# High and low part as one operand of 512 columns in six output stages of a two-block transformer kernel

## The chip, the cores and the metric

The kernel runs on one core of a Trainium2 chip. The metric is the time of one execution in device microseconds. TensorE multiplies matrices, VectorE and ScalarE work elementwise, GpSimd and SyncE issue DMAs. TensorE's results land in PSUM, in banks of 512 numbers of 32 bits per partition.

## The reference

Two blocks of two layers each on 256 tokens of width 1024 (the first block's first layer also carries 256 context tokens). Layer by layer there are attention or a state-space mixer, an output projection, and an MLP; all in float32. What matters here are the products that are added to the residual h:

```python
h_lat = h_lat + ga1 * y_lat                     # y_lat = attention(...) @ swa_wo[j]
h_lat = h_lat + ga2 * squared_relu_mlp(modulate(rms_norm(h_lat, g_mlp[i]), sh2, sc2), mlp_w1[i], mlp_w2[i])
...
h = h + sb_mixer(rms_norm_2(h, b_norm[j]), b_w_q[j], b_q_norm[j], k, v, b_w_o[j])
h = h + conv_ffn(rms_norm_2(h, ffn_norm[layer]), ffn_w_up[layer], ffn_conv_w[layer], ffn_conv_b[layer], ffn_w_down[layer])
```

## The kernel before, in words

Channels lie on the 128 partitions, tokens along the columns. A weight matrix is cut into units of 1024 columns (512 KB): eight k-tiles of 128 x 128 for one output tile of 128 channels. All weights run in one order through a ring of four slots.

Precision comes from two parts: each float32 number x is split into a rounded part "hi" (type float32r) and the rest "lo". A product is hi*hi + w_hi*x_lo + w_lo*x_hi, three matmuls into the same columns of one bank (`products`, L724 to L732), each with a weight load of its own. With 256 tokens only half of the bank is used.

For each weight unit SyncE loads `raw` (`load_unit`), ScalarE rounds it to `w_hi` (`split_unit`, L1144; it waits until TensorE is done with the slot's last unit), VectorE subtracts to get `w_lo` (`lower`, L1576), TensorE waits for that (`lo`). ScalarE and VectorE run their queues strictly in order, so this work stands in one line with the work on the output tiles.

Stages are of kinds. "RES" stages are output projections whose result is added to h. Those on 256 tokens are wo1, wo2 (8 tiles of one unit, 8 k-tiles each), down1a, down1b (8 tiles of two units, 16 k-tiles) and fdown0, fdown1 (8 tiles of three units, 22 k-tiles). The order of the stages from wo1 on: wo1, norm, up1a, down1a, up1b, down1b, win, state-space mixer, glu, fup0, fdown0, k2, q2, v2, attention, wo2, fup1, fdown1, output. Tiles use banks 0 to 3 in turn; TensorE may start tile j when h of tile j - 4 has been updated.

In a RES stage VectorE does, per tile: the `lower` of the units that come three later (the one of every fourth tile's last unit after the tile, in stages with row sums), then the update of h (L1621 to L1635). wo1, down1a and down1b have a gate: one scalar_tensor_tensor, h = bank * gate + h (L1633). wo2 has none (L1629), and fdown0 and fdown1 first multiply the bank by `rsn` (L1628), then add. Stages with row sums (wo1, down1b, fdown0, wo2) go on per tile: ScalarE waits for h, makes the next stage's high operand (`next_hi`, L1243, not in wo1) and the square of h (L1187), and after these the next `split_unit`; VectorE makes the low operand (`next_lo`, L1672) and adds the square to `ssum` (L1717). At the end TensorE sums `ssum` and the last square over the channels (`row_total`, L828): for wo1 before the norm, for the others after the sixth k-tile of the next stage.

In down1a, up1b and down1b VectorE also makes tables for the state-space mixer (`tables`, L2096 to L2105), in parts at fixed units; TensorE multiplies them at fixed units too (`table_mid`, L638 and L651), two units after the part in these stages. A `link` is a semaphore increment by an instruction and a wait for it by the next one on the same engine.

fup1 (kind "UP") may start its first tile when the second last update of h in wo2 is done (`bank_free`).

## Time and profile before

| | |
|---|---|
| median of 3 runs (1707.87 to 1715.15) | 1713.21 us |
| span of the profiled execution | 1706.6 us |
| TensorE matmul busy | 1606.4 us, 94%, 11872 instructions |
| TensorE weight load busy | 1421.1 us, 83% |
| VectorE busy | 1308.7 us, 77%, 2229 instructions |
| ScalarE busy | 869.5 us, 51% |
| mean granted clock of TensorE | 0.982 |
| chain that ended last | PE 73%; DVE 18%; issue 4%; ACT 3%; DMA 2% |

PE is TensorE, DVE VectorE, ACT ScalarE. The span runs from the first to the last instruction of one execution that the profiler took; the runs' times are of other executions and hold what lies around the span too. Matmuls are pipelined: their durations overlap, so what one costs is read from the distance between two starts. The granted clock is the share of full speed (2.4 GHz) that TensorE was given; half of it is 1.2 GHz. "Idle before" is the idle time of the engine just before an instruction, with who ended it.

### The profile page before, as it was taken

How to read it: one execution, taken by the hardware profiler on the slowest of the kernel's cores; microseconds unless marked ns; L12 is line 12 of the kernel's file. 1: busy time of each engine (PE TensorE's matmuls, PEld its weight loads, DVE VectorE, ACT ScalarE, POOL GpSimd, SP SyncE). 2: the span in 40 equal slices, each digit the busy share in tenths (PEclk: the TensorE clock that was granted, in tenths of full speed). 3: DMA queues.
4: the chain of work that ended last, by engine and by line, in shares of the span. 5: the costliest groups of instructions: out<-in, count | busy, mean ns of one | idle time of the engine just before them, and what ended most of it. 6: DMA issues, size and time to landing. Idle time of an engine off the chain costs nothing.

```text
span 1706.6 us, 32698 instructions
## 1 busy us (share of the span) xinstructions
PE 1606.4 (94%) x11872; PEld 1421.1 (83%) x11872; DVE 1308.7 (77%) x2229; ACT 869.5 (51%) x1505; POOL 104.3 (6%) x174
## 2 busy tenths in 40 slices
PE   6999899899999999788989999889999999899999
PEld 3778666688888888674789999789999998699999
DVE  5899897788767867678677787777887686578874
ACT  4664386343213433566555555355555586555542
POOL 0001030000000023120000212000000000000000
PEclk9999999999999999998999999999999999999999
DMA  9246651345667855340156667735555644055554
GB/s 368 89 137 224 218 149 51 123 144 184 202 193 238 263 173 169 112 140 12 53 186 202 217 208 263 316 102 176 179 183 177 205 153 158 13 164 183 182 196 137
DMA packets 80828, 292.02 MB, mean 171 GB/s; under 512 B 10432, under 2 KB 12224, under 8 KB 78928
## 3 DMA queue, kind: packets, MB, share of 16 engines
q1 hardware_dynamic: 69552, 249.03, 44.4%
q0 software_dynamic: 11168, 41.54, 7.6%
q8 instruction: 69, 1.13, 0.3%
q14 instruction: 39, 0.32, 0.1%
HBM read 270.54 MB, written 18.68 MB: 169 GB/s over the span
## 4 chain that ended last, share of the span: by engine, by line
PE 73%; DVE 18%; issue 4%; ACT 3%; DMA 2%; ACTq 0%; DVEq 0%; SPq 0%; POOLq 0%
PE bank L730 22%; PE bank L732 21%; PE bank L731 21%; DVE stat L2121 2%; DVE w_lo L1576 2%; DVE prob L2140 1%; PE bank L914 1%; DVE bank L1588 1%; DVE ada_raw L1589 1%; PE bank L925 1%; DMA raw<-weights 1%; PE bank L940 1%; DVE qk L1771 1%; DMA ada_raw<-ada_w 1%; PE bank L818 1%
## 5 line engine op out<-in xcount | busy, mean ns | idle before, releaser
L730 PE MATMUL bank<-u_hi,w_hi 128*128 128x256 f32 (+1 forms) x1936 | 615.9, 318 | 31.2 <-DVE u_lo L1951 19.2
L731 PE MATMUL bank<-u_lo,w_hi 128*128 128x256 f32 (+1 forms) x1936 | 600.8, 310 | 0.0
L732 PE MATMUL bank<-u_hi,w_lo 128*128 128x256 f32 (+1 forms) x1936 | 600.8, 310 | 0.0
L1576 DVE TENSOR_TENSOR w_lo<-raw,w_hi 128x1024 fp32r<-128x1024 f32 x372 | 452.2, 1222 | 143.9 <-ACT w_hi L1144 131.4
L1144 ACT ACTIVATE w_hi<-raw 128x1024 fp32r<-128x1024 f32 x360 | 375.4, 1049 | 172.8 <-PE bank L732 142.7
L730 PEld LDWEIGHTS bank<-u_hi,w_hi 128*128 128x128 f32 x1936 | 372.5, 192 | 59.6 <-issue 35.7
L731 PEld LDWEIGHTS bank<-u_lo,w_hi 128*128 128x128 f32 x1936 | 372.8, 193 | 22.3 <-issue 3.8
L732 PEld LDWEIGHTS bank<-u_hi,w_lo 128*128 128x128 f32 x1936 | 372.6, 192 | 18.4
L730 PE MATMUL bank<-hid_hi,w_hi 128*128 128x512 f32 (+1 forms) x512 | 174.0, 340 | 0.0
L732 PE MATMUL bank<-hid_hi,w_lo 128*128 128x512 f32 (+1 forms) x512 | 172.1, 336 | 0.0
L731 PE MATMUL bank<-hid_lo,w_hi 128*128 128x512 f32 (+1 forms) x512 | 172.0, 336 | 0.0
L730 PEld LDWEIGHTS bank<-hid_hi,w_hi 128*128 128x128 f32 x512 | 97.1, 190 | 11.0 <-issue 1.5
L732 PEld LDWEIGHTS bank<-hid_hi,w_lo 128*128 128x128 f32 x512 | 97.1, 190 | 10.2
L731 PEld LDWEIGHTS bank<-hid_lo,w_hi 128*128 128x128 f32 x512 | 97.1, 190 | 9.7
L1589 DVE SCALAR_TENSOR_TENSOR ada_raw<-ada_raw,silu_row 128x1024 f32<-128x1024 f32 x80 | 97.7, 1222 | 9.3 <-DMA ada_raw<-ada_w 9.0
L730 PE MATMUL bank<-f_hi,w_hi 128*128 128x256 f32 x352 | 99.8, 283 | 0.0
L731 PE MATMUL bank<-f_lo,w_hi 128*128 128x256 f32 x352 | 99.6, 283 | 0.0
L732 PE MATMUL bank<-f_hi,w_lo 128*128 128x256 f32 x352 | 99.6, 283 | 0.0
L1195 ACT ACTIVATE rs<-bank 128x512 f32<-128x512 f32 (+1 forms) x64 | 31.3, 489 | 125.2 <-PE bank L732 118.7
L730 PEld LDWEIGHTS bank<-f_hi,w_hi 128*128 128x128 f32 x352 | 67.6, 192 | 0.2
L732 PEld LDWEIGHTS bank<-f_hi,w_lo 128*128 128x128 f32 x352 | 67.6, 192 | 0.0
L731 PEld LDWEIGHTS bank<-f_lo,w_hi 128*128 128x128 f32 x352 | 67.6, 192 | 0.0
(317 smaller groups left out, 2260.3 us busy)
## 6 DMA issues: line engine op xcount, KB each, us to landing
raw<-weights SPq DMA_DIRECT2D x372, 512.0 KB, 3.4
ada_raw<-ada_w SPq DMA_DIRECT2D x80, 512.0 KB, 4.1
ada_first<-ada_w SPq DMA_DIRECT2D x16, 512.0 KB, 14.4
bias_sb<-bias_na POOLq DMA_DIRECT2D x16, 256.0 KB, 3.4
toep_dram<-zeros POOLq DMA_DIRECT2D x8, 512.0 KB, 9.1
bat_dram<-bat POOLq DMA_DIRECT2D x16, 256.0 KB, 4.2
ca_dram<-ca POOLq DMA_DIRECT2D x16, 256.0 KB, 3.8
s_bat<-bat_dram POOLq DMA_DIRECT2D x4, 1024.0 KB, 8.2
```

What stands on the lines that cost most here:

```text
L730: pe.matmul(dst, wh, hi[:, kt, xs], start=first, stop=False)
L731: pe.matmul(dst, wh, lo[:, kt, xs], start=False, stop=False)
L732: return pe.matmul(dst, wl, hi[:, kt, xs], start=False, stop=final)
L818: pe.matmul(SUM_BANKS[b2][:, 0:s.tok], C("block"), sq[:, b2, 0:s.tok], start=True, stop=True).then_inc(S["p2"], 1)
L914: pe.matmul(psum[2 * (g % 2) + a][:, 0:keys], q_ap, k_ap, start=True, stop=True).then_inc(att_s, 1)
L925: mm = pe.transpose(psum[4 + a][:, t * P:(t + 1) * P], prob[:, 2 * (g % 2) + a, t * P:(t + 1) * P], C("ident"))
L940: mm = pe.matmul(psum[6 + pr % 2][a * HD:(a + 1) * HD, qt * P:(qt + 1) * P], heads[a][2][t], prob_t[:, 2 * (g % 2) + a, t * P:(t + 1) * P] ...
L1144: A(w_hi[:, slot, :], raw[:, slot, :], ACT.Copy).then_inc(S["hi"], 1)
L1195: chain.link(A(rs[:, b2, 0:s.tok], bank[:, 0:s.tok], ACT.Relu))
L1576: TT(w_lo[:, slot, :], raw[:, slot, :], w_hi[:, slot, :].bitcast(F32), ALU.subtract).then_inc(S["lo"], 1)
L1589: STT(raw_, raw_, 1.0, silu_row[:, 0, :], ALU.mult, ALU.mult, accum_out=ada_acc[:, b, a % 4, 0:1]).then_inc(S["ada_read"], 1)
L2121: red = dve.tensor_reduce(stat[:, 0, b, :], both[:, :, 0:keys], AX.X, ALU.max, negate=True)
```

## The change

In the six RES stages of 256 tokens the high and the low operand are addressed as one tensor with a leading dimension of two (`u_both`, `hid1_both`, `f_both`; the addresses stay the same). Under the high weight one matmul takes both, 2 x 256 columns, into the whole bank; the low weight's matmul adds hi's product to the upper half. So a k-tile has two matmuls and two weight loads in place of three and three. The two halves of the bank are added when h is updated: VectorE adds the upper half's product to h and then the lower half's, in two instructions with a link between them. In fdown0 and fdown1 the multiplication by `rsn` takes the whole bank of 512 columns, and two additions follow, both linked to what is before them.

```diff
--- before.py
+++ after.py
@@ -181,8 +181,8 @@
         big = cursor[0]
         cursor[0] += 64 * 1024
         u_at = cursor[0]
-        u_hi = place("u_hi", [P, KT, TOK], F32R)
-        u_lo = place("u_lo", [P, KT, TOK], F32R)
+        u_both = place("u_both", [P, 2, KT, TOK], F32R)
+        u_hi, u_lo = u_both[:, 0], u_both[:, 1]
         con = place("con", [P, N_CON])
         vec = place("vec", [P, N_VEC])
         adab = place("adab", [P, 2, N_ADA, 2])
@@ -234,8 +234,8 @@
         sb_w = place("sb_w", [P, 2, 2, 384], at=at_ + 6144)
         mask_r = place("mask_r", [P, 384], F32R, at=big + 40960)
         ident_r = place("ident_r", [P, P], F32R, at=big + 42496)
-        f_hi = place("f_hi", [P, FT, SEQ], F32R, at=big)
-        f_lo = place("f_lo", [P, FT, SEQ], F32R, at=big + FT * 1024)
+        f_both = place("f_both", [P, 2, FT, SEQ], F32R, at=big)
+        f_hi, f_lo = f_both[:, 0], f_both[:, 1]
         fx = big + 2 * FT * 1024
         f_c = place("f_c", [P, 2, SEQ], at=fx)
         f_sig = place("f_sig", [P, 2, SEQ], at=fx + 2048)
@@ -265,8 +265,8 @@
 
         HOME0 = table_home("0", u_at, (sq_at + 4096, sq_at + 12288), PAIRS // 2)
         HOME1 = table_home("1", big + 32768, (big + 32768 + 25600, big + 32768 + 30208), PAIRS // 2)
-        hid1_hi = place("hid1_hi", [P, HALF, SEQ], F32R, at=big)
-        hid1_lo = place("hid1_lo", [P, HALF, SEQ], F32R, at=big + 16384)
+        hid1_both = place("hid1_both", [P, 2, HALF, SEQ], F32R, at=big)
+        hid1_hi, hid1_lo = hid1_both[:, 0], hid1_both[:, 1]
         HID = {n: (hid_hi, hid_lo) for n in ("up0a", "up0b")}
         HID.update({n: (hid1_hi, hid1_lo) for n in ("up1a", "up1b")})
         assert cursor[0] <= nc.sbuf_usable_end, cursor[0] - nc.sbuf_usable_end
@@ -482,6 +482,7 @@
                     "v2": (("q2", ("a1", "a3")),)}
 
         MODS_NEEDED = {"mix0": 4, "mlp0": 10, "mix1": 16, "mlp1": 22}
+        BOTH = {"wo1": u_both, "wo2": u_both, "down1a": hid1_both, "down1b": hid1_both, "fdown0": f_both, "fdown1": f_both}
         VAL = {"v0": val0, "v1": val1, "v2": val2}
         QK_DST = {"qk0": qk0, "q1": q1, "k1": k1, "k2": k2, "q2": q2}
         QK_GAIN = {"qk0": ("gqk0", 0), "q1": ("gqk1", 0), "k1": ("gqk1", 8), "k2": ("gqk2", 0), "q2": ("gqk2", 8)}
@@ -727,6 +728,11 @@
                 wh, wl = w_hi[:, slot, t * P:(t + 1) * P], w_lo[:, slot, t * P:(t + 1) * P]
                 dst = TILE[(s.tile0 + jj) % RING][:, 0:s.tok]
                 xs = NORM_COLS.get(s.name, slice(0, s.tok))
+                if s.name in BOTH:
+                    bank = TILE[(s.tile0 + jj) % RING]
+                    pe.matmul(bank[:, :].rearrange("p (a t) -> p a t", a=2), wh, BOTH[s.name][:, :, kt, xs], start=first, stop=False,
+                              skip_group_check=True)
+                    return pe.matmul(bank[:, SEQ:2 * SEQ], wl, hi[:, kt, xs], start=False, stop=final, skip_group_check=True)
                 pe.matmul(dst, wh, hi[:, kt, xs], start=first, stop=False)
                 pe.matmul(dst, wh, lo[:, kt, xs], start=False, stop=False)
                 return pe.matmul(dst, wl, hi[:, kt, xs], start=False, stop=final)
@@ -1621,12 +1627,19 @@
                 elif s.kind == "RES":
                     dve.wait_ge(S["unit"], n_done)
                     gate = s.more.get("gate")
+                    lower_half = slice(SEQ, 2 * SEQ)
                     if gate is None:
                         part = bank
                         if s.name in HIDDEN:
                             part = tmp[:, b2, :]
-                            link(TT(part[:, all_], bank[:, all_], rsn[:, all_], ALU.mult))
+                            link(TT(part.rearrange("p (a t) -> p a t", a=2), bank[:, :].rearrange("p (a t) -> p a t", a=2),
+                                    rsn[:, all_].unsqueeze(1).to_broadcast([P, 2, SEQ]), ALU.mult))
+                        link(TT(dcol(h, j, all_), part[:, lower_half], dcol(h, j, all_), ALU.add))
                         TT(dcol(h, j, all_), part[:, all_], dcol(h, j, all_), ALU.add).then_inc(S["d1"], 1)
+                    elif s.name in BOTH:
+                        g = mod[:, gate[0], bass.ds(j + gate[1] * 8, 1), 0]
+                        link(STT(dcol(h, j, all_), bank[:, lower_half], g, dcol(h, j, all_), ALU.mult, ALU.add))
+                        STT(dcol(h, j, all_), bank[:, all_], g, dcol(h, j, all_), ALU.mult, ALU.add).then_inc(S["d1"], 1)
                     else:
                         for hf in range(s.tok // SEQ):
                             cs = slice(hf * SEQ, (hf + 1) * SEQ)
```

## Rows read from the trace of the kernel before

**Rows 1.** Busy time by stretch: wo1, down1a, down1b, wo2, fdown1. PE, PEld, DVE, ACT, POOL, clock, DMA.

```profile
834.90:858.30 23.40, 23.29 (x192) 23.09 (x192) 13.73 (x21) 9.15 (x15) 0.00 (x0) 1.00 0.44 137
...
912.80:962.30 49.50, 49.50 (x468) 48.81 (x467) 39.40 (x50) 23.47 (x38) 10.38 (x17) 1.00 0.71 224
...
1009.80:1057.70 47.90, 47.90 (x428) 47.52 (x427) 34.85 (x50) 24.59 (x42) 8.88 (x15) 1.00 0.66 213
...
1486.80:1510.20 23.40, 23.29 (x192) 23.09 (x192) 14.01 (x24) 10.71 (x19) 0.00 (x0) 1.00 0.41 135
...
1639.80:1703.40 63.60, 63.57 (x529) 63.36 (x528) 34.91 (x44) 23.66 (x25) 0.00 (x0) 1.00 0.53 170
```

**Rows 2.** TensorE in order of time, down1a. Start, duration, line, operands, idle before.

```profile
949.74 0.28 PE L732 MATMUL bank<-hid_hi,w_lo 128*128 128x256 f32 x1
...
959.10 0.28 PE L732 MATMUL bank<-hid_hi,w_lo 128*128 128x256 f32 x1
```

**Rows 3.** TensorE in order of time, down0a, 512 columns.

```profile
439.69 0.39 PE L732 MATMUL bank<-hid_hi,w_lo 128*128 128x512 f32 x1
...
445.81 0.39 PE L732 MATMUL bank<-hid_hi,w_lo 128*128 128x512 f32 x1
```

**Rows 4.** VectorE in order of time, wo2.

```profile
1507.03 0.42 DVE L1629 TENSOR_TENSOR h<-bank,h 128x256 f32<-128x256 f32 x1
...
1509.57 1.23 DVE L1576 TENSOR_TENSOR w_lo<-raw,w_hi 128x1024 fp32r<-128x1024 f32 x1 [1.39 <-ACT w_hi L1144]
...
1510.71 0.42 DVE L1629 TENSOR_TENSOR h<-bank,h 128x256 f32<-128x256 f32 x1
```

**Rows 5.** TensorE in order of time, first and fifth tile of fup1.

```profile
1511.18 0.39 PE L730 MATMUL bank<-u_hi,w_hi 128*128 128x256 f32 x1 [1.03 <-DVE h L1629]
...
1524.42 0.36 PE L730 MATMUL bank<-u_hi,w_hi 128*128 128x256 f32 x1 [0.40 <-DVE f_h L1737]
```

**Rows 6.** VectorE in order of time, wo1.

```profile
853.78 0.48 DVE L1633 SCALAR_TENSOR_TENSOR h<-bank,mod,h 128x256 f32<-128x256 f32 x1
...
857.00 0.48 DVE L1633 SCALAR_TENSOR_TENSOR h<-bank,mod,h 128x256 f32<-128x256 f32 x1
...
858.31 0.48 DVE L1633 SCALAR_TENSOR_TENSOR h<-bank,mod,h 128x256 f32<-128x256 f32 x1 [0.50 <-PE bank L732]
```

**Rows 7.** VectorE in order of time, two linked instructions on 255 and 254 columns.

```profile
1522.72 0.48 DVE L1732 SCALAR_TENSOR_TENSOR f_c<-f_g,vec,f_c 128x255 f32<-128x255 f32 x1
...
1523.24 0.48 DVE L1734 SCALAR_TENSOR_TENSOR f_c<-f_g,vec,f_c 128x254 f32<-128x254 f32 x1
```

**Rows 8.** VectorE in order of time, two linked tensor_tensor, fdown0.

```profile
1339.94 0.42 DVE L1628 TENSOR_TENSOR tmp<-bank,rsn 128x256 f32<-128x256 f32 x1
...
1340.39 0.43 DVE L1629 TENSOR_TENSOR h<-tmp,h 128x256 f32<-128x256 f32 x1
```

**Rows 9.** VectorE by line and form: name, count, busy, mean ns, idle.

```profile
L2205 DVE TENSOR_TENSOR x_mod<-bank,rot 128x512 f32<-128x512 f32 x4 | 2.7, 677 | 1.4 <-PE bank L1012 1.4
```

**Rows 10.** VectorE in order of time, down1b.

```profile
1033.92 0.48 DVE L1633 SCALAR_TENSOR_TENSOR h<-bank,mod,h 128x256 f32<-128x256 f32 x1 [0.29 <-PE bank L732]
...
1039.51 0.76 DVE L2103 SCALAR_TENSOR_TENSOR ca<-ca,tab_tmp 128x576 f32<-128x576 f32 x1
```

**Rows 11.** TensorE in order of time, down1b, unit 10.

```profile
1040.33 0.54 PE L651 MATMUL bank<-ca,tab_bbar 64*16 64x128 f32 x23
```

**Rows 12.** Busy time by stretch: around the start of up1a, and an idle stretch.

```profile
860.40:864.60 4.20, 0.00 (x0) 0.00 (x0) 3.17 (x8) 1.75 (x4) 0.20 (x1) 0.72 0.95 316
...
864.60:871.60 7.00, 6.96 (x42) 6.99 (x43) 5.83 (x14) 4.01 (x7) 0.00 (x0) 0.68 0.21 81
...
1082.50:1084.80 2.30, 0.01 (x2) 0.01 (x1) 1.81 (x3) 2.07 (x3) 0.47 (x1) 1.00 0.93 360
```

**Rows 13.** VectorE in order of time, start of k2.

```profile
1364.82 0.42 DVE L1717 TENSOR_TENSOR ssum<-ssum,sq 128x256 f32<-128x256 f32 x1
```

**Rows 14.** TensorE in order of time, row totals in k2.

```profile
1365.58 0.60 PE L828 MATMUL bank<-ssum,con 128*128 128x256 f32 x2
```

## Prediction

> **What bounds the kernel now.** I read three views. First the busy time of each engine, stage by stage [rows 1]: in five of the six stages that change (fdown0 is built like fdown1) TensorE is busy for the whole stretch, VectorE for 55 to 80% of it, the DMA engines for 41 to 71%. Second the order of time on TensorE [rows 2, 3]. What counts there is the distance between starts, since the durations overlap. With 256 columns, 949.74 to 959.10 us is 78 distances, 120.0 ns each. With 512 columns, 439.69 to 445.81 us is 27 distances, 226.7 ns each. The difference is 106.7 ns for 256 columns, which is 2.4 GHz. So every matmul with its weight load costs its columns and 13.3 ns besides. Third, the joints between stages, in order of time on VectorE and TensorE [rows 4 to 6, 10, 11]. They show what the share of busy time hides: in wo1 and wo2 a chain of VectorE and ScalarE is longer than TensorE's tile. The result update of a tile (h) lets ScalarE square h; only then, in its queue, does it split the next weight unit; VectorE subtracts the low part (1.23 us) and only then reaches the next tile's h. Updates of h stand 3.68 us apart in wo2 (1507.03 to 1510.71) and 3.22 us apart in wo1 (853.78 to 857.00), where TensorE needs 24 matmuls of 120 ns, 2.88 us. At the end of wo2 TensorE has run out of lead and waits 1.03 us for the second last h [rows 5].
>
> **What is removed on TensorE.** Per k-tile three pairs of load and matmul (360.0 ns) become one of 512 and one of 256 columns (226.7 + 120.0 = 346.7 ns). The columns stay, one fixed cost of 13.3 ns goes. K-tiles: wo1 and wo2 64 each, down1a and down1b 128 each, fdown0 and fdown1 176 each, 736 in all, 9.8 us if all of it arrived.
> No row shows a moving operand in two pieces (high and low lie apart). Bounds: nothing, as the 512 columns in one piece show [rows 3], or one more fixed cost of 13.3 ns, as if it were two matmuls. A gain has no reason, since each column must stream. I take nothing, the nearest row being the one of the same count of columns.
> The Trainium skill (TensorE: Matmul & The Clock Gate, "Back-to-back issue gap") gives an isolated gap of N/2.4 + 2.5 ns; by that the change would save 736 x 2.5 ns, an estimate of 1.8 us, not 9.8. The rows here show 13.3 ns at both widths, so the rule does not hold for these loads and matmuls; the forecast doesn't use it.
>
> **What is added on VectorE.** A gated update (wo1, down1a, down1b) gets a second scalar_tensor_tensor, linked to the first by a semaphore. Two such linked instructions start 0.52 us apart [rows 7]. In wo2 it is a second linked tensor_tensor; linked ones start 0.45 us apart [rows 8]. In fdown0 and fdown1 the scaling takes 512 columns in place of 256 (677 ns from PSUM, where 256 took 0.42 us [rows 8, 9], so +0.26 us) and a linked add, 0.45 us: +0.7 us a tile. The read of rsn twice over is taken at no cost, as the table operations that repeat an operand show nothing else at 512 columns; its upper bound would be another 0.3 us at two joints.
>
> **Stage by stage**, against the profiled execution.
> down1a: TensorE-bound [rows 1], VectorE 39.4 of 49.5 us busy; 8 x 0.52 = 4.2 us more leave it under 44 of 47.8 us. This stage takes no row sums, so ScalarE doesn't wait for h. All of the gain arrives: 128 x 13.3 ns = -1.7 us.
> down1b: here ScalarE does wait for h, and VectorE also makes the last state-space table, which TensorE needs in its unit 10. The table's last part ends at 1039.51 + 0.76 = 1040.27 us, TensorE takes it at 1040.33 us: no slack [rows 10, 11]. Three updates of h lie ahead of the fourth in that chain, 3 x 0.52 = 1.56 us, less 0.29 us that VectorE waited for TensorE there; with the fourth's own 0.52 us the table comes 1.8 us later. TensorE comes 82 k-tiles x 13.3 ns = 1.1 us earlier and stalls some 2.9 us. The stage gives +1.8 us up to there and -0.6 us on its last 46 k-tiles: +1.2 us. Bounds: -1.7 us, if the chain has slack between its tiles that I didn't see, and +1.8 us.
> wo1: the first update starts 0.1 us earlier (8 k-tiles). Up to the eighth update the chain has seven links of 0.52 us, 3.6 us; but the fourth tile's update waited for TensorE and its row sum for a square, and the eighth's waited 0.50 us for TensorE again, some 1.4 us of slack in all. 3.6 - 0.1 - 1.4: the last row sum comes 2.1 us later, and the norm and up1a wait for it. TensorE's 0.85 us are lost in this. +2.1 us; bounds +1.0 (half of the links hidden) and +3.1 (all eight links, 4.2 us, less 1.1 us).
> wo2: the same chain with 0.45 us a step. Seven links up to the end of the second last h are 3.2 us, less 0.1 us at the first tile and 0.5 us at the fourth, whose square is next on ScalarE only after a weight split and so hides one link: that h ends 2.6 us later, so fup1 starts 2.6 us later. The chain stays the last to end up to the fifth tile of fup1, where TensorE waits 0.40 us for VectorE [rows 5], so nothing is caught up. +2.6 us; bounds +1.3 and +3.4.
> The clock at that joint: wo2's last matmul would end 0.85 us earlier and fup1 start 2.6 us later, so TensorE's idle 1.03 us becomes some 4.5 us. In this trace, TensorE's idle stretch before up1a (4.3 us) came with the granted clock down to half, and in the 7 us after it the mean grant was 0.68; a stretch of 2.3 us left it at 1.00 [rows 12]. 0.68 means 4.5 us of the 7 at 1.2 GHz, where 256 columns take 213 ns (256 / 1.2 GHz) in place of 120: 44% of 4.5 us, 2.0 us, less the 0.40 us that TensorE waited there anyway: +1.6 us. I take it, as 4.5 us is nearer to 4.3 than to 2.3.
> fdown0: TensorE-bound, VectorE has room: 176 x 13.3 ns = -2.35 us. At its end the row totals need the last-but-one row sum, which ended at 1365.24 us, 0.34 us before TensorE took it [rows 13, 14]; 0.7 us more makes a stall of 0.4 us. -1.95 us.
> fdown1: -2.35 us, and the last tile's chain to the output +0.7 us in the open: -1.65 us.
> What moves otherwise: nothing; the operands keep their addresses, and no DMA or queue is passed. Each bank is freed 0.5 us later, with three further banks before TensorE wants it again.
>
> **Sum**: -1.7 + 1.2 + 2.1 + 2.6 + 1.6 - 1.95 - 1.65 = +2.2 us. The profiled span of 1706.6 us becomes 1708.8 us. The median of the runs, 1713.2 us, lies 6.6 us above the span; the same difference gives 1715.4 us. (A measurement of this kernel can tell about 0.5%, 8.6 us, from no change.)
>
> **Rivals.**
> The gain arrives whole: VectorE's additions are hidden, as its 77% of busy time suggests, except the last tile's 0.7 us: -9.8 + 0.7 gives 1704.1 us, just faster. Against it stand the steps of 3.68 and 3.22 us [rows 4, 6].
> The clock stays up at fup1: 1713.8 us. For it: the grant depends on more than the length of the gap.
> The clock falls also at the 2.9 us stall in down1b: 2.0 us more, 1717.4 us. Against it: the gap lies between a stretch of 2.3 us that was harmless and 4.3 us.
> Slower: the split operand. If each read in two pieces costs x more, TensorE pays 526 x, over the k-tiles where it is on the path (128 in down1a, 46 in down1b, 352 in fdown). At x = 13.3 ns that is 7.0 us, 1722.4 us, slower by 0.5%; it decides from x = 12 ns. For it: no row has such an operand. Against it: the cost of a matmul in this trace is columns and a fixed part.
> The two-figure rule of the page named above (2.5 ns) would be a rival of the same kind, with 19% of the gain on the path: 5.7 us of the 7.0 lost, 1721.1 us. I give it 0.03, since 120.0 and 226.7 ns speak against it.
>
> **How the numbers follow.** Forecast as summed 0.60; clock stays up 0.14; gain arrives whole 0.06; clock falls in down1b too 0.08; split operand 0.09; small fixed cost 0.03. Predicted: 1715.4 us. The forecast's own bounds: low with wo1 and wo2 at their lower ends and no stall in down1b, 1715.4 - 1.1 - 1.3 - 2.9 = 1710.1; high with the upper ends, 1715.4 + 0.9 + 0.8 + 0.6 = 1717.7. The runs of before spread by 5.3 us below and 1.9 us above their median, so I widen to 1707 below; above, I reach to the split operand, 1722.5. Faster 0.06, slower 0.10, within 0.5% 0.84.
>
> **What would show each step.** On TensorE: starts in the pattern 227 and 120 ns in fdown1, 61.2 us in place of 63.6 for the stage; 240 and 120 would be the split operand. On VectorE: updates of h 4.1 us apart in wo2 and 3.7 us in wo1; an idle stretch of TensorE of some 4.5 us ahead of fup1 with the granted clock at half behind it; a wait of TensorE for ca in down1b of about 2.9 us; the row total of wo1 2.1 us later relative to the stage's start. The forecast is wrong if wo1 and wo2 end when TensorE does, or if down1b runs through.

## The result and the profile after

| | median | runs | ratio to before |
|---|---|---|---|
| before | 1712.32 us | 16 | |
| after | 1719.25 us | 16 | 1.0041, interval 1.0031 to 1.0052 |

The change costs 7.0 us (interval 5.3 to 8.9 us). The forecast was 1715.4 us. The profiled execution of after spans 1716.8 us, in a run of 1718.94 us. So 2.1 us lie around a span, not the 6.6 us that the forecast carried along.

The table gives, from the order of time on TensorE, what each stage costs from its first start to the next stage's first start (in the last row, up to the end of the span), as the difference after minus before in microseconds. The first pair is the two traces that the case began with; the second pair is a further execution of each kernel (e9 and e11 below).

| stage | forecast | first pair | second pair |
|---|---|---|---|
| wo1 to the start of up1a | +2.1 | +2.11 | +2.03 |
| up1a (clock) | 0 | +0.57 | +0.56 |
| down1a | -1.7 | -1.03 | -1.06 |
| down1b | +1.2 | +1.39 | +1.38 |
| end of win to the start of glu | 0 | +3.61 | +2.77 |
| glu | 0 | +1.38 | +1.58 |
| fdown0 | -2.35 | -2.33 | -2.33 |
| k2 (wait for the row sum) | +0.4 | +0.72 | +0.73 |
| wo2 to the start of fup1 | +2.6 | +2.71 | +2.65 |
| fup1 (clock) | +1.6 | +0.58 | +0.63 |
| fdown1, and the chain to the output | -1.65 | -1.24 + 0.70 | -1.23 + 0.73 |

Without the two lines from win to glu these add up to +4.2 us (first pair) where +2.2 was forecast. The remaining 2.8 of the 7.0 us must lie where nothing was changed. Between the end of win and the end of glu both pairs show more than that, 5.0 and 4.4 us, but a third kernel with the whole change (e3) shows 1.2 us there, and much of it varies between executions, as told below. Other unchanged stages differ either way (the spans of the pairs differ by 10.2 and 6.0 us).

Busy time by stretch, kernel after, for wo1, down1a, down1b, wo2 (both up to the next stage's start) and fdown1; columns as in [rows 1]:

```profile
835.12:867.70 32.58, 23.73 (x133) 20.33 (x133) 23.42 (x42) 12.57 (x20) 2.03 (x3) 0.93 0.50 172
916.40:964.70 48.30, 48.30 (x339) 41.61 (x338) 42.59 (x57) 23.50 (x38) 10.25 (x16) 1.00 0.68 226
1012.30:1061.40 49.10, 46.94 (x298) 40.48 (x298) 38.10 (x57) 24.39 (x42) 8.88 (x15) 1.00 0.59 192
1493.60:1522.20 28.60, 23.75 (x134) 20.49 (x135) 19.31 (x36) 11.93 (x21) 0.00 (x0) 0.99 0.36 116
1650.60:1712.70 62.10, 62.10 (x353) 53.74 (x351) 38.53 (x51) 23.79 (x25) 0.00 (x0) 1.00 0.49 168
```

down1a and fdown1 are shorter than in [rows 1] and TensorE is still busy throughout: there the saved time arrives. down1b was run through before; now TensorE is idle for 2.16 of its 49.1 us and the stage is longer.

TensorE in order of time, after, in fdown0 and in fdown1:

```profile
1321.79 0.39 PE L733 MATMUL bank<-f_both,w_hi 128*128 128x512 f32 x1
1322.02 0.28 PE L735 MATMUL bank<-f_both,w_lo 128*128 128x256 f32 x1
1322.13 0.39 PE L733 MATMUL bank<-f_both,w_hi 128*128 128x512 f32 x1
...
1689.72 0.40 PE L733 MATMUL bank<-f_both,w_hi 128*128 128x512 f32 x1
1689.95 0.28 PE L735 MATMUL bank<-f_both,w_lo 128*128 128x256 f32 x1
1690.07 0.40 PE L733 MATMUL bank<-f_both,w_hi 128*128 128x512 f32 x1
1690.31 0.28 PE L735 MATMUL bank<-f_both,w_lo 128*128 128x256 f32 x1
1690.43 0.40 PE L733 MATMUL bank<-f_both,w_hi 128*128 128x512 f32 x1
```

In fdown0 the starts of one k-tile are 0.34 us apart, again and again: 230 + 117 = 347 ns, the forecast's sum. In fdown1 they are 0.35 and 0.36 us apart, by turns 241 + 120, 236 + 113 and 233 + 117 ns, 353 ns on average. So only half of the saving arrives there, and in down1a too.

VectorE in order of time, after: two updates of h in wo1, two in wo2 (each update is two instructions now, the rows are of the second), and the state-space table in down1b:

```profile
852.49 0.48 DVE L1642 SCALAR_TENSOR_TENSOR h<-bank,mod,h 128x256 f32<-128x256 f32 x1
...
856.24 0.48 DVE L1642 SCALAR_TENSOR_TENSOR h<-bank,mod,h 128x256 f32<-128x256 f32 x1
...
1043.73 0.76 DVE L2116 SCALAR_TENSOR_TENSOR ca<-ca,tab_tmp 128x576 f32<-128x576 f32 x1
...
1512.57 0.42 DVE L1638 TENSOR_TENSOR h<-bank,h 128x256 f32<-128x256 f32 x1
1515.11 1.22 DVE L1582 TENSOR_TENSOR w_lo<-raw,w_hi 128x1024 fp32r<-128x1024 f32 x1 [2.11 <-ACT w_hi L1150]
...
1516.70 0.42 DVE L1638 TENSOR_TENSOR h<-bank,h 128x256 f32<-128x256 f32 x1
```

Updates stand 4.13 us apart in wo2 and 3.75 us in wo1; 3.68 and 3.22 us were read before [rows 4, 6]. So the link's 0.45 to 0.53 us is paid in full at each of these steps, because VectorE waits for ScalarE's next weight split and that waits for h.

TensorE in order of time, after: at that table, at the first row total in k2, and at the joint from wo2 to fup1; then the busy time of three stretches, the end of the idle stretch and the start of up1a, the idle stretch ahead of fup1 and what follows that (the clock is the third figure from the end):

```profile
1044.54 0.33 PE L652 MATMUL bank<-ca,tab_bbar 64*16 64x128 f32 x8 [2.16 <-DVE ca L2116]
...
1372.57 0.48 PE L834 MATMUL bank<-ssum,con 128*128 128x256 f32 x1 [0.29 <-DVE ssum L1730]
...
1516.88 0.28 PE L735 MATMUL bank<-u_both,w_lo 128*128 128x256 f32 x1
1521.32 0.39 PE L736 MATMUL bank<-u_both,w_hi 128*128 128x256 f32 x1 [4.16 <-DVE h L1638]
```

```profile
862.00:872.50 10.50, 6.08 (x27) 5.58 (x28) 8.91 (x21) 4.70 (x11) 0.00 (x0) 0.55 0.49 176
...
1517.20:1521.40 4.20, 0.08 (x1) 0.08 (x1) 2.77 (x6) 1.76 (x3) 0.00 (x0) 1.00 0.37 125
1521.40:1526.00 4.60, 4.60 (x23) 4.50 (x24) 4.30 (x9) 3.41 (x6) 0.00 (x0) 0.63 0.34 114
```

The idle 1.03 us [rows 5] have become 4.16 us, and the granted clock behind them is 0.63 on average over 4.6 us, partly at 1.2 GHz. Ahead of up1a it is the same: 0.55 over the 10.5 us that hold the idle stretch's end and the stage's start, where 0.68 and 0.72 stood before [rows 12].

The table that came just in time [rows 10, 11] now keeps TensorE idle for 2.16 us, and in k2 TensorE waits for a row sum that was there before [rows 13, 14].

### The profile page after: what moved, and what is told of

Its sections match the earlier page's. It is cut to its first block, busy times and chain, and to the rows that moved or that the text cites. A ratio compares the mean times of both kernels' runs of the same rounds, so it can differ in the third digit from the quotient of the medians.

```text
span 1716.8 us, 31306 instructions
## 1 busy us (share of the span) xinstructions
PE 1604.1 (93%) x11136; PEld 1386.8 (81%) x11136; DVE 1332.5 (78%) x2277; ACT 870.5 (51%) x1505; POOL 104.3 (6%) x174
## 3 DMA queue, kind: packets, MB, share of 16 engines
q8 instruction: 65, 1.06, 0.3%
## 4 chain that ended last, share of the span: by engine, by line
PE 69%; DVE 20%; ACT 4%; issue 4%; DMA 2%; ACTq 0%; DVEq 0%; SPq 0%; POOLq 0%
PE bank L736 17%; PE bank L737 16%; PE bank L738 16%; PE bank L733 7%; PE bank L735 4%; DVE w_lo L1582 3%; DVE stat L2134 2%; DMA raw<-weights 1%; DVE prob L2153 1%; DVE bank L1594 1%; DVE ada_raw L1595 1%; ACT w_hi L1150 1%; PE bank L920 1%; PE bank L931 1%; PE bank L946 1%
## 5 line engine op out<-in xcount | busy, mean ns | idle before, releaser
L736 PE MATMUL bank<-u_both,w_hi 128*128 128x256 f32 (+1 forms) x1808 | 581.8, 322 | 32.9 <-DVE u_both L1964 18.8
L737 PE MATMUL bank<-u_both,w_hi 128*128 128x256 f32 (+1 forms) x1808 | 566.7, 313 | 0.0
L738 PE MATMUL bank<-u_both,w_lo 128*128 128x256 f32 (+1 forms) x1808 | 566.6, 313 | 0.0
L736 PEld LDWEIGHTS bank<-u_both,w_hi 128*128 128x128 f32 x1808 | 350.1, 194 | 61.0 <-issue 33.1
L737 PEld LDWEIGHTS bank<-u_both,w_hi 128*128 128x128 f32 x1808 | 350.3, 194 | 22.3 <-issue 3.8
L738 PEld LDWEIGHTS bank<-u_both,w_lo 128*128 128x128 f32 x1808 | 350.0, 194 | 18.7
L733 PE MATMUL bank<-f_both,w_hi 128*128 128x512 f32 x352 | 123.4, 395 | 0.0
L736 PE MATMUL bank<-hid_hi,w_hi 128*128 128x512 f32 x256 | 100.8, 394 | 0.0
L738 PE MATMUL bank<-hid_hi,w_lo 128*128 128x512 f32 x256 | 99.7, 390 | 0.0
L737 PE MATMUL bank<-hid_lo,w_hi 128*128 128x512 f32 x256 | 99.7, 389 | 0.0
L735 PE MATMUL bank<-f_both,w_lo 128*128 128x256 f32 x352 | 98.7, 280 | 0.0
L733 PE MATMUL bank<-hid_both,w_hi 128*128 128x512 f32 x256 | 91.5, 401 | 0.0
```

The lines of the kernel that those rows point to most:

```text
L733: pe.matmul(bank[:, :].rearrange("p (a t) -> p a t", a=2), wh, BOTH[s.name][:, :, kt, xs], start=first, stop=False, skip_group_check=True)
L735: return pe.matmul(bank[:, SEQ:2 * SEQ], wl, hi[:, kt, xs], start=False, stop=final, skip_group_check=True)
L736: pe.matmul(dst, wh, hi[:, kt, xs], start=first, stop=False)
L737: pe.matmul(dst, wh, lo[:, kt, xs], start=False, stop=False)
L738: return pe.matmul(dst, wl, hi[:, kt, xs], start=False, stop=final)
```

## The experiments

Ratios are to the kernel before on the same chip; its medians were 1712.37 us for e1 to e4, 1711.52 us for e5 to e8 and 1711.70 us for e9 to e12.

**e1 and e2: the two halves of the change alone.** e1 leaves TensorE as before and gives VectorE the added instructions (their addend is the bank times 0, so that nothing is added; the excerpt shows the stages without a gate):

```diff
-    link(TT(part[:, all_], bank[:, all_], rsn[:, all_], ALU.mult))
+    link(TT(part.rearrange("p (a t) -> p a t", a=2), bank[:, :].rearrange("p (a t) -> p a t", a=2),
+            rsn[:, all_].unsqueeze(1).to_broadcast([P, 2, SEQ]), ALU.mult))
+    link(STT(dcol(h, j, all_), part[:, all_], 0.0, dcol(h, j, all_), ALU.mult, ALU.add))
     TT(dcol(h, j, all_), part[:, all_], dcol(h, j, all_), ALU.add).then_inc(S["d1"], 1)
```

> TensorE as in the kernel before (three matmuls of 256 columns); VectorE as after the change, with the added linked instruction in all six stages multiplying by 0 so that h stays the same. Theory A (the link on the chain of VectorE and ScalarE costs): +2.2 us at the end of wo1, +2.7 us at the end of wo2 with up to 2 us more for TensorE's clock, +1.8 us in down1b at the last table, +0.4 and +0.7 us after fdown0 and fdown1: 8 to 10 us over before. Theory B (VectorE's additions are hidden and what the change lost it lost on TensorE, by the operand in two pieces): only the last tile's 0.7 us and at most 1 us besides.

e2 has TensorE as after and VectorE as before; the upper half of the bank, w_hi*x_lo and w_lo*x_hi, is left out of h (the excerpt shows the stages with a gate).

```diff
-    link(STT(dcol(h, j, all_), bank[:, lower_half], g, dcol(h, j, all_), ALU.mult, ALU.add))
     STT(dcol(h, j, all_), bank[:, all_], g, dcol(h, j, all_), ALU.mult, ALU.add).then_inc(S["d1"], 1)
```

> TensorE as after the change, VectorE as before: the upper half of the bank is not added, so w_hi*x_lo and w_lo*x_hi are left out of the six stages' results. Theory A: down1a and down1b -1.7 us each at 346.7 ns a k-tile (-0.85 each at 353 ns), fdown0 and fdown1 -2.35 us each (-1.2 at 353 ns), wo1 and wo2 together -0.5 us since the chain without links is already longer than TensorE's tile: -5 to -8.6 us. Theory B: within 2 us of before.

e1: 1720.27 us, ratio 1.0047 (1.0032 to 1.0063). e2: 1708.48 us, ratio 0.9975 (0.9964 to 0.9987). VectorE's part alone costs 7.9 us, as much as the whole change; TensorE's part alone gains 3.9 us, less than the 5 to 8.6 us expected. The two add up to 4.0 us, not to the change's 7.0. One reason is that in wo1, wo2 and up to the table in down1b TensorE's gain is worth nothing once VectorE is late: in e1 the way from wo2's first start to fup1's is 27.08 us, after 27.03 us. By stages, 1.9 of the 3.0 us can be placed: 0.8 in wo1, 0.6 in down1b and 1.0 in up1a, less 0.5 in fup1, all against the first trace of before. up1a takes only 47.52 us in e1 (before 48.19, after 48.76); less of it ran at the lower clock. The rest isn't placed. In e2 the way from wo2 to fup1 is 24.23 us, 0.1 us less than before: even with nothing added, ScalarE's and VectorE's chain sets the end of wo2. The six changed stages of e2's trace give -5.8 us together, and the clock at fup1 takes 0.6 us of that back.

TensorE at that joint in e2, and the busy time around it:

```profile
1510.41 0.28 PE L735 MATMUL bank<-u_both,w_lo 128*128 128x256 f32 x1
1512.47 0.38 PE L736 MATMUL bank<-u_both,w_hi 128*128 128x256 f32 x1 [1.78 <-DVE h L1636]
```

```profile
1510.60:1512.40 1.80, 0.10 (x1) 0.00 (x0) 1.54 (x3) 0.23 (x1) 0.00 (x0) 1.00 0.27 109
1512.40:1519.40 7.00, 6.93 (x42) 6.82 (x43) 5.33 (x11) 4.70 (x9) 0.00 (x0) 0.76 0.45 151
```

TensorE ends 0.84 us sooner and waits 1.78 us in place of 1.03, and the clock falls behind even this short wait (0.76 over 7 us). From its first to its last start fup1 takes 129.06 us, as after (before 128.41). So here a faster TensorE ahead of an unchanged chain buys a longer wait and a slower clock.

**e3: the split operand.** High and low lie next to each other in hid1 and f, so that the 512 columns are one piece in four of the six stages.

```diff
-        f_both = place("f_both", [P, 2, FT, SEQ], F32R, at=big)
+        f_both = place("f_both", [P, FT, 2, SEQ], F32R, at=big)
...
+                        pe.matmul(bank[:, :], wh, BOTH[s.name][:, kt].rearrange("p a t -> p (a t)"), start=first, stop=False,
+                                  skip_group_check=True)
```

> The change whole, but in down1a, down1b, fdown0 and fdown1 high and low of a k-tile lie next to each other, so the operand is one piece of 512 columns. If two pieces cost TensorE (after shows starts of 241/120, 236/113, 233/117 ns in down1a and fdown1, 353 ns a k-tile, but 347 in fdown0 and wo1), all four stages show 346.7 ns a k-tile and the kernel is 2 to 3 us faster than after (some +4.5 us over before). If the pieces don't matter, the mix of 347 and 353 stays and the time is that of after, +7 us.

1719.66 us, ratio 1.0044 (1.0030 to 1.0058): as after. From first to last start down1a takes 48.16 us and fdown1 62.07 us, both as after to 0.01 us. That rules out the rival of the split operand: reading it in two pieces costs nothing, and the 353 ns a k-tile don't come from it. On the contrary, fdown0 takes 62.15 us here (353 ns), where after has 60.97. The layout isn't what does that: e4 below, with after's fdown0 and after's layout, has 62.14 us too.

**e4, e7, e8: single stages.** e4 keeps the change in down1a, fdown0 and fdown1 alone, e7 in wo1 and wo2, e8 in down1b; all three are of this form (VectorE's update of h goes by the same list):

```diff
-        BOTH = {"wo1": u_both, "wo2": u_both, "down1a": hid1_both, "down1b": hid1_both, "fdown0": f_both, "fdown1": f_both}
+        BOTH = {"down1a": hid1_both, "fdown0": f_both, "fdown1": f_both}
```

> The change in down1a, fdown0 and fdown1 alone, where VectorE has room. Theory A: -1.7 or -0.85, -1.95 and -1.65 or -0.5 us: 3.3 to 5.3 us faster than before. Theory B (the loss lies with the operand, wherever it is used): no faster than before.

> The change in wo1 and wo2 alone. Theory A: +2.1 us at wo1, +2.7 us at wo2, and 0.6 us of lower clock at the start of fup1: +5.4 us over before, most of what the whole change loses. If clock phases elsewhere are behind the whole loss, it is near 0.

> The change in down1b alone. Theory A: TensorE waits for the last table (ca) and the stage is 1.4 us longer: +1.4 us over before. If the links are hidden there: -0.7 to -1.7 us.

e4: 1710.40 us, 0.9989 (0.9977 to 1.0001). e7: 1720.33 us, 1.0046 (1.0029 to 1.0062). e8: 1714.22 us, 1.0011 (1.0000 to 1.0022). In e4's trace the three stages are 1.03, 1.16 and 1.18 us shorter than before (each at some 353 ns a k-tile), k2 is 0.72 us longer; that is -2.7 us before the output's 0.7 us, and -2.0 us was measured (3.3 to 5.3 us had been expected). The interval reaches 1.0001, so the time alone doesn't show this gain; the stages do. e7 was expected at +5.4 us and gave +8.8 us. Its stages give +2.08 (wo1), +0.61 (clock in up1a), +2.67 (wo2) and +0.61 us (clock in fup1), together 6.0; the stretch from win to glu, which it doesn't touch, is 3.1 us longer than in the first trace of before. e8's median is 2.7 us above before's, where 1.4 was expected, and its down1b is 2.69 us longer in its trace, since there the clock fell behind the wait for the table. TensorE in e8, and the busy time behind the wait:

```profile
1043.93 0.66 PE L652 MATMUL bank<-ca,tab_bbar 64*16 64x128 f32 x32 [2.19 <-DVE ca L2120]
```

```profile
1044.00:1050.00 6.00, 6.00 (x54) 5.05 (x55) 3.11 (x4) 4.01 (x12) 1.10 (x2) 0.72 0.60 209
```

The same wait, 2.16 us in after and 2.19 us here, left the clock at 1.00 there and brought it to 0.72 here. This is the rival "the clock falls also in down1b": it happens in some executions.

**e5, e6, e10: the order on ScalarE.** If the chain h, square, weight split, low part, next h is what bounds wo1 and wo2, it is cut by letting ScalarE split the next tile's first unit before the work that waits for h. e5 does so in the kernel after, in the four stages with row sums; e6 in the kernel before; e10 is e5's kernel once more.

```diff
+                early = row_sums(s) and s.tok == SEQ
...
-                            if not last:
+                            if early and k == 0 and i * body + jj > 0:
+                                pass
+                            elif not last:
                                 split_unit(s, i, n, per)
...
+                        if early and s.kind == "RES" and i * body + jj < s.tiles - 1:
+                            split_unit(s, i, (jj + 1) * s.units, per)
                         tile(s, i, jj, body, first)
...
-                    for i in turns(act, s, s.tiles // body, chain, n_links):
+                    for i in turns(act, s, s.tiles // body, chain, n_links, (*TABLES, *WHOLE, "wo1", "wo2", "fdown0")):
                         one(i)
```

The change to `turns` also writes out ScalarE's loop of two passes in wo1, wo2 and fdown0. No run has the order without it.

> The change whole, and in wo1, wo2, down1b and fdown0 ScalarE splits the first weight unit of the next tile ahead of the work on h (next high operand and square) instead of behind it. So a link in the update of h no longer delays the next low weight. Theory A (the chain update of h - square - weight split - low weight carries the links): wo1 from start to up1a 31.75 us becomes 29.5 to 30.5, wo2 to fup1 27.03 us becomes about 24, down1b 49.0 becomes 47 to 48; 4 to 6 us faster than after, about +2 us over before. Theory C (VectorE is simply full in these stages, its own busy time carries them): the stages stay within 0.5 us of what they are after the change.

> The kernel before with the same reordering of ScalarE alone, as the reference for the one above. Theory A: wo2 to fup1 24.32 us becomes 23.2 and wo1 to up1a stays within 0.5 us of 29.65; 1 to 2 us faster than before. Theory C: no difference.

> e5 once more, on the same chip as the kernel after (e9) and with the same runs of the kernel before, so that the two can be compared directly. Theory: 1707.8 us, ratio to before 0.9976 within 0.001, and 11.4 us (0.66%) below e9; of this 1.3 to 2.4 us in wo1's end, 4.7 us in wo2's end, some 2 us in down1b, the rest the clock at fup1. Rival (e5 came out low by the luck of its chip): at or above 0.9990.

e5: 1707.81 us, 0.9976 (0.9966 to 0.9986). e10: 1706.26 us, 0.9964 (0.9952 to 0.9976), in the same batch as after, which stood at 1719.52 us: 13.3 us less, 11.4 expected. Of e5 4 to 6 us less than after had been expected; -3.7 us against before, where after has +7.0, is some 11 us. e6: 1708.59 us, 0.9984 (0.9974 to 0.9994), 2.9 us less than before where 1 to 2 were expected, with no wait left ahead of fup1 (24.32 us became 23.13) and down1b 0.44 us longer. In e5 TensorE goes from wo2 into fup1 without a wait, and the steps between updates of h that take 4.13 to 4.16 us in after take 1.92 to 2.78 us. These steps lie inside a pass of four tiles, so the written-out loop doesn't explain them. TensorE, then VectorE in order of time, e5:

```profile
1507.97 0.28 PE L735 MATMUL bank<-u_both,w_lo 128*128 128x256 f32 x1
1508.09 0.28 PE L736 MATMUL bank<-u_both,w_hi 128*128 128x256 f32 x1
```

```profile
1504.13 0.42 DVE L1644 TENSOR_TENSOR h<-bank,h 128x256 f32<-128x256 f32 x1
...
1506.79 0.42 DVE L1644 TENSOR_TENSOR h<-bank,h 128x256 f32<-128x256 f32 x1
```

From wo2's first start to fup1's it is 22.29 us (after 27.03, before 24.32), fup1 takes 128.43 us (first to last start), as before, with the clock up, wo1 to up1a takes 29.33 us (after 31.76, before 29.65), and down1b 47.15 us (after 49.01). These three places make 9.0 us (4.74, 2.43 and 1.86), the clock behind two of them 1.0 us more. Two stages whose TensorE work isn't touched moved as well: fup0 is 0.8 us shorter in all four traces with this edit, e6's among them (130.5 for 131.4 us), and fdown0 is 1.2 us longer than in after (353 ns a k-tile for 347). With this order the full change beats the kernel before, by 3.7 us (e5) and 5.4 us (e10). Most of that is the order's own: e6 against before is 2.9 us. e5 against e6 says what the change itself brings then: 0.8 us by the medians, which these intervals don't tell from nothing.

**e9 and e11: the same kernels once more**, after and before unchanged, to see what repeats.

> The kernel after once more, unchanged, beside the one with the earlier split (e10). Theory: the cost of a pair (512 + 256 columns), 346.7 or some 353 ns, is not fixed by the program but falls out anew in each execution; then the stages down1a, fdown0, fdown1, wo1 and wo2 show 48.16, 60.97 or 62.15, 62.07, 22.17 or 22.59 us here in another arrangement than before (in the first trace of this kernel: 353 in down1a, wo2, fdown1, 346.7 in fdown0, wo1). Rival: it is fixed by the program, and every stage repeats its length to 0.1 us. Time, both: 1719.3 us, ratio 1.0041 within 0.001.

> The kernel before once more, for a second profiled execution. Theory: the profiled execution that the prediction read was a fast one by 3.6 us; a run's time lies 2.1 us above its span in every run, so the span here is 1706 to 1713 us, and its time 2.1 us more. The stages that differ in length from the first profile are those with half clock: q1 (34.4 or 35.9 us), up0a (88.3 or 89.6), the stretch from win to glu (37.5 to 41 us), glu (49.6 or 51.0). Rival: the 6.6 us between span and median lie in every execution, then span and time of this run differ by 6.6 us.

e9: 1719.52 us, 1.0048 (1.0029 to 1.0067). e11: one run of 1712.06 us with a span of 1709.9 us, 2.1 us around it. So the profiled execution that the forecast started from (1706.6 us) was a quick one, by 3.3 us against e11 and by 3.6 us against before's median less 2.1 us. The two traces of before differ in stages that the change doesn't touch, q1 (34.36 or 35.85 us from first to last start), up0a (88.26 or 89.81 us); all six changed stages agree to 0.02 us. The theory that a k-tile costs 347 or 353 ns by chance in each execution mostly fell: down1a, fdown0 and fdown1 repeat their 48.16, 60.97 and 62.07 us to 0.01 us, though fdown0 and fdown1 run the same instructions. wo2 did change, 22.59 us in the first trace and 22.32 us in the second, and in the two executions of the other kernel (e5, e10) it has 22.17 and 22.59 us.

**e12: the order of the two matmuls.** e10's kernel with the low weight's 256 columns first in every second k-tile, so that equal widths come in twos.

```diff
+                    if kt % 2:
+                        pe.matmul(bank[:, SEQ:2 * SEQ], wl, hi[:, kt, xs], start=False, stop=False, skip_group_check=True)
+                        return pe.matmul(bank[:, :].rearrange("p (a t) -> p a t", a=2), wh, BOTH[s.name][:, :, kt, xs], start=False,
+                                         stop=final, skip_group_check=True)
```

> e10's kernel, but in every second k-tile of the six stages the low weight's 256 columns go first and the high weight's 512 columns second, so that the matmuls run 512, 256, 256, 512, 512, 256, 256, 512. Theory: the 353 ns that a pair costs in some stages come from the strict change of 512 and 256 columns (each weight load hides under the matmul ahead of it, and a long one and a short one take turns); with pairs of equal length every pair costs 346.7 ns or the pattern goes: down1a 47.5 in place of 48.16 us, fdown0 and fdown1 60.97 in place of 62.1, 1704.5 us in all. Rival (the order has nothing to do with it): the stage lengths are again either of the two values, 1707.8 us. Third: a load ahead of the 512 columns behind another 512 doesn't hide as well: above 353 ns a pair, slower than e10 by 736 x the difference.

TensorE in order of time, e12, fdown1:

```profile
1689.74 0.40 PE L735 MATMUL bank<-f_both,w_hi 128*128 128x512 f32 x1
1689.97 0.39 PE L737 MATMUL bank<-f_both,w_hi 128*128 128x512 f32 x1
1690.20 0.28 PE L739 MATMUL bank<-f_both,w_lo 128*128 128x256 f32 x1
1690.32 0.28 PE L734 MATMUL bank<-f_both,w_lo 128*128 128x256 f32 x1
1690.43 0.40 PE L735 MATMUL bank<-f_both,w_hi 128*128 128x512 f32 x1
```

Two k-tiles take 0.69 to 0.70 us here, 348 ns each, in all three long stages. From start to start of the neighbouring stages down1a, down1b, fdown0 and fdown1 are 0.3, 0.5, 0.9 and 0.9 us shorter than in e10: the order of the widths moves the price. It isn't all that sets it, since in strict alternation fdown0 has 347 ns in after and 353 ns in e10, the one below and the other above the 348 ns here. The time didn't follow: 1706.45 us, 0.9974 (0.9963 to 0.9986), against e10's 1706.26 us. 2.6 us less was to be seen and 0.2 us more was measured (1.7 us more by the two ratios); the intervals are 2 us wide to each side, so this neither shows the gain nor excludes most of it.

**The stretch from win to glu.** No run was made for it alone, but all traces show it. Around the last weight splits ahead of the state-space mixer: ScalarE in order of time and the busy time of win, of after and then of e11 (before once more).

```profile
1086.39 1.06 ACT L1150 ACTIVATE w_hi<-raw 128x1024 fp32r<-128x1024 f32 x1 [2.73 <-DMA raw<-weights]
1088.93 1.06 ACT L1150 ACTIVATE w_hi<-raw 128x1024 fp32r<-128x1024 f32 x1 [1.48 <-DMA raw<-weights]
1090.01 1.28 ACT L1482 ACT_TABLE_LOAD   x1
```

```profile
1061.50:1085.30 23.80, 23.80 (x198) 23.69 (x197) 15.89 (x23) 7.79 (x10) 2.08 (x4) 1.00 1.00 406
```

```profile
1084.56 1.06 ACT L1144 ACTIVATE w_hi<-raw 128x1024 fp32r<-128x1024 f32 x1 [2.76 <-DMA raw<-weights]
1085.88 1.06 ACT L1144 ACTIVATE w_hi<-raw 128x1024 fp32r<-128x1024 f32 x1 [0.26 <-DMA raw<-weights]
1086.95 1.28 ACT L1476 ACT_TABLE_LOAD   x1
```

```profile
1060.80:1084.60 23.80, 23.80 (x198) 23.69 (x196) 15.64 (x22) 7.83 (x11) 2.09 (x4) 1.00 1.01 417
```

During win the DMA engines are busy for all of the time (share 1.00 and 1.01), and ScalarE waits for each unit's DMA. The last of these units is split 3.67 us after win's last matmul starts in after (1085.26 us), and 1.28 us after it in e11 (1084.59 us); ScalarE's work for the mixer is queued behind it. In the first trace of before the lag is 1.83 us, so in the two pairs it grew by 1.8 us, and the stretch by 3.6 and 2.8 us. Over all fourteen traces this lag and the length of the stretch go together, if not strictly: with a lag under 2 us (before, e11, e5, e6, e8, e12) the stretch is 37.4 to 39.2 us, with 2 to 3 us (e2, e3, e10) 38.8 to 40.3 us, with more (after, e9, e1, e4, e7) 38.9 to 41.2 us. It isn't the wait in down1b that does it: e4 and e7 leave down1b as it is and stand at 40.9 and 40.6 us. All kernels but e6 are above the two traces of before here, by 0.4 to 3.6 us. But part of this is not the kernel's: e5 and e10, the same kernel, have 39.20 and 40.27 us, and e3, with the whole change, 38.79 us. The mean granted clock doesn't order them either (0.95 over before's stretch, 0.91 over after's, 0.85 over e3's). Which shift of earlier work makes the last unit late wasn't tried and stays open.

**glu.** TensorE starts the fifth k-tile of glu 6.3 to 6.5 us into the stage in every trace, when VectorE has made its low operand. TensorE in order of time and the busy time behind that wait, of after and then of e3:

```profile
1132.84 0.58 PE L736 MATMUL bank<-u_both,w_hi 128*128 128x256 f32 x1 [2.04 <-DVE u_both L2252]
...
1133.44 0.42 PE L738 MATMUL bank<-u_both,w_lo 128*128 128x256 f32 x1
1133.65 0.41 PE L736 MATMUL bank<-u_both,w_hi 128*128 128x256 f32 x1
```

```profile
1132.80:1136.10 3.30, 3.26 (x15) 3.26 (x16) 1.71 (x2) 0.00 (x0) 0.00 (x0) 0.50 0.12 27
```

```profile
1130.27 0.39 PE L740 MATMUL bank<-u_both,w_hi 128*128 128x256 f32 x1 [1.07 <-DVE u_both L2256]
...
1130.61 0.28 PE L742 MATMUL bank<-u_both,w_lo 128*128 128x256 f32 x1
1130.73 0.28 PE L740 MATMUL bank<-u_both,w_hi 128*128 128x256 f32 x1
```

```profile
1130.20:1133.50 3.30, 3.23 (x27) 3.23 (x28) 1.73 (x3) 0.41 (x1) 0.00 (x0) 1.00 0.14 32
```

In after, e9, e2 and e8 the wait is 1.85 to 2.06 us, the clock is at half behind it (starts 0.21 us apart), and glu takes 51.1 to 51.2 us. In the other ten traces the wait is 0.88 to 1.71 us, starts stand 0.12 us apart and glu takes 49.7 us. Four of these ten, e3, e5, e10 and e12, have the whole change. So glu's 1.4 to 1.6 us are the clock's, and the change doesn't bring them in every execution.

## Why the prediction was right, and where it was off

**The sign and the size.** "Within 0.5%, a little slower" was forecast, and the time, 1719.25 us, is 0.41% above before and within the range. It is 3.9 us above the forecast; the steps say why. That it lies within the range is luck in part: with every step at its upper bound the forecast ends at 1717.7 us, and the range reaches to 1722.5 only for the split operand, a rival that e3 refutes. Of the 7.0 us that the change costs, the sum has 2.2.

**The chains in wo1 and wo2, right.** The count of seven links, less the slack at the fourth and the eighth tile, gave +2.1 and +2.6 us; +2.11 and +2.71 us were measured. The steps of 3.7 and 4.1 us between updates came as 3.75 and 4.13 us. e1, with TensorE as before, has +1.71 and +2.76 us, so they are VectorE's in the main, and e5 and e10 show that it is the order of ScalarE's queue that puts them on the path. The rival "gain arrives whole" fell: nothing of it arrives in wo1, wo2 and the first part of down1b.

**down1b, right.** A wait of 2.9 us and +1.2 us for the stage were forecast, 2.16 us and +1.39 us measured. The rival of a slower clock behind it came true in e8 and not in after or e9. The wait is shorter and the stage longer by what TensorE didn't gain: the k-tiles ahead of the table cost 353 ns, not 346.7.

**The gain per k-tile, off by half in places.** The step "226.7 + 120.0 = 346.7 ns" holds in fdown0 (-2.33 us) and wo1. In down1a and fdown1 the term was mis-sized, -1.03 and -1.24 us in place of -1.7 and -2.35. The two distances were read from stretches of equal matmuls [rows 2, 3] and added, and a sequence that changes between them was taken at the sum. e3 shows that the pieces of the operand aren't the cause, and e12 that the order of widths moves the price; why strict alternation costs 347 ns in one stage and 353 in another stays open. Together 1.8 us were missing. No stage saves as little as the 2.5 ns of the last rival.
The Trainium skill (TensorE: Matmul & The Clock Gate, "Back-to-back issue gap") gives N/2.4 + 2.5 ns for an isolated matmul; by that such a k-tile would take 512/2.4 + 256/2.4 + 2 x 2.5 = 325 ns, an estimate. No changed stage here averages below 346 ns.

**The clock at fup1, mechanism right, size off.** It fell behind the idle stretch as forecast (4.16 us, 4.5 forecast), but fup1 lost 0.58 us, not 1.6. The price was taken over from the joint before up1a, where the clock stayed low for longer: 0.63 over 4.6 us is 3.4 us at 1.2 GHz, and 4.5 us were taken. And more of it was hidden: up to its fifth tile fup1 takes 12.38 us where TensorE waits for nothing (e6), 13.24 before and 13.98 after. So the clock costs 1.6 us there, and TensorE had lost 0.86 of them before already, not only the 0.40 us that were taken off. That same joint was forgotten on the other side: wo1's idle stretch grew as well, and up1a became 0.57 us longer. Both clock terms together are 1.2 us, and 1.6 us stood in the sum.

**k2, step right, a little more behind it.** The last-but-one row sum is late as costed: at the row total the distance between two starts is 0.57 us where 0.12 was due, a wait of 0.45 us. The other 0.27 us of the stage stand behind it, which the step had not: 0.10 at the next matmul of the row total (0.32 for 0.22 us) and 0.16 ahead of k2's own first sum (0.28 for 0.12 us).

**"What moves otherwise: nothing", wrong.** It is the largest miss: 2.8 to 3.6 us between win and glu in the two pairs, and some 1.5 us in glu. The DMA share of 0.41 to 0.71 was read for the stages that change [rows 1]; win, where it is 1.00 and where ScalarE waits for each weight unit, wasn't looked at. An arrival 1.8 us later there puts ScalarE's work for the mixer 1.8 us later; for the rest of that stretch no cause is shown. glu's part is a slower clock behind a wait. That the change causes either isn't shown: both traces of after have them, but e3, the whole change as well, has 1.2 us between win and glu and nothing in glu.

**The offset, wrong but without effect.** The 6.6 us between the profiled span and the median were taken as lying around the span. It is 2.1 us in e11 and in after; the rest was a quick execution. Since the forecast added the difference to the same median, its change of +2.2 us stood as it was.

## What to carry to other kernels

A saving on the busiest engine is worth something only in the stages where no chain through other engines is as long as its tile: look at the distance between the results, not at busy shares. Before adding an instruction behind a result, look at who waits for that result in strict queue order; here the order of one ScalarE instruction decided between 7 us lost and 4 to 5 us won, of which the order brings 2.9 us without the change. And where a later stretch waits for DMA, look at when its last transfer lands, in more than one execution, before calling it untouched.

## What the runs showed of the hardware

- A 512-column matmul of 241 to 230 ns and a 256-column one of 120 to 112 ns alternate in fixed patterns; a k-tile of both costs 346.7 or 353 ns in strict alternation, 348 ns with equal widths in twos. Two stages with the same matmuls (fdown0 and fdown1 of after) differ, and do so again in a second execution; the same fdown0 costs 353 ns when other stages are changed (e4), and wo2 varied between executions of one kernel. What picks the price isn't known.
- A moving operand in two pieces of 256 columns costs the same as 512 in one piece (48.16 us for down1a and 62.07 us for fdown1, both ways).
- The clock fell to half behind an idle stretch of 1.8 us (e2). Behind 2.16 us it stayed up in one kernel (after) and behind 2.19 us it fell in another (e8). At one place in glu it was at half behind 1.85 to 2.06 us in four traces, and up behind 0.88 to 1.71 us in ten. So a short wait isn't safe by its length, and rows of one trace [rows 12] don't settle it.
